# Hybrid diffusion step on one core: where the attention probabilities are normalised

## The reference, cut to what matters

```python
def attend(q, k, v, mask, sink):
    s = jnp.einsum('bqkgd,bskd->bkgqs', q.astype(F32), k.astype(F32)) * (HEAD_DIM ** -0.5)
    if mask is not None:
        s = jnp.where(mask, s, -jnp.inf)
    sk = sink.astype(F32)[None, :, :, None, None]
    m = jnp.maximum(jnp.max(s, axis=-1, keepdims=True), sk)
    e = jnp.exp(s - m)
    prob = e / (jnp.sum(e, axis=-1, keepdims=True) + jnp.exp(sk - m))
    o = jnp.einsum('bkgqs,bskd->bqkgd', prob, v.astype(F32))
    return o.astype(q.dtype)
```

## Time and profile before

| | |
|---|---|
| median of 3 runs | 2896.82 us (2895.7 to 2900.62) |
| the profiled execution | 2894.71 us, its span 2892.9 us |
| TensorE busy | 92% of the span |
| VectorE busy | 43% |
| ScalarE busy | 28% |
| GpSimd busy | 9% |
| DMA, mean | 74 GB/s |

### The profile page before, as it was taken

The page is one execution under the profiler, slowest core; times in us unless marked ns, Lnnn a source line. Parts: engine busy times, 40 slices in busy tenths (PEclk is TensorE's granted clock), DMA queues, the critical chain, the costliest instruction groups (busy, mean ns, idle before and its releaser), DMA issues.

```text
span 2892.9 us, 38685 instructions
## 1 busy us (share of the span) xinstructions
PE 2675.1 (92%) x16849; PEld 2314.2 (80%) x16849; DVE 1252.3 (43%) x1978; ACT 801.5 (28%) x1234; POOL 264.3 (9%) x174
## 2 busy tenths in 40 slices
PE   6989897889999899999988998788999998999998
PEld 4946445679999799999977564385899988999997
DVE  3495646452233422223356756636422343223224
ACT  5222122352224522112252211224321244221212
POOL 0020412000111000000001204210001110000000
PEclk8989998899999999999999999988999999999999
DMA  6021003223323032323302010122232221222221
GB/s 241 19 78 44 29 15 90 73 75 117 96 81 102 17 104 88 103 93 98 91 30 78 4 59 15 44 75 75 80 124 89 83 78 41 77 66 81 69 88 41
DMA packets 214622, 213.42 MB, mean 74 GB/s; under 512 B 29480, under 2 KB 205040, under 8 KB 214070
## 3 DMA queue, kind: packets, MB, share of 16 engines
q1 hardware_dynamic: 214454, 210.95, 23.2%
HBM read 207.52 MB, written 3.41 MB: 73 GB/s over the span
## 4 chain that ended last, share of the span: by engine, by line
PE 81%; DVE 12%; ACT 4%; issue 2%; POOL 1%; DMA 1%; SPq 0%; DVEq 0%; ACTq 0%
PE ps L622 54%; PE ps L581 6%; DVE arena L1614 4%; PE ps L605 3%; PE ps L1100 3%; PE ps L593 3%; PE ps L672 1%; PE ps L882 1%; DVE arena L1715 1%; PE ps L1010 1%; ACT normed L723 1%; DVE normed L748 1%; PE ps L1165 1%; PE ps L1260 1%; ACT arena L2081 1%
## 5 line engine op out<-in xcount | busy, mean ns | idle before, releaser
L622 PE MATMUL ps<-arena_parts,weights_parts 128*128 128x320 f32 x8416 | 1428.9, 309 | 3.6 <-DVE normed_parts L1689 3.6
L622 PEld LDWEIGHTS ps<-arena_parts,weights_parts 128*128 128x128 f32 x8416 | 1275.8, 187 | 19.2 <-DVE normed_parts L1689 4.4
L539 DVE TENSOR_TENSOR weights_parts<-weights,weights_parts 128x2048 fp32r<-128x2048 f32 (+2 forms) x140 | 285.5, 2039 | 772.5 <-ACT weights_parts L531 772.5
L622 PE MATMUL ps<-normed_parts,weights_parts 128*128 128x320 f32 x2240 | 510.0, 309 | 0.0
L622 PEld LDWEIGHTS ps<-normed_parts,weights_parts 128*128 128x128 f32 x2240 | 376.1, 188 | 0.0
L531 ACT CAST weights_parts<-weights 128x2048 fp32r<-128x2048 f32 (+2 forms) x140 | 232.5, 1660 | 267.8 <-PE ps L622 171.5
L581 PE MATMUL ps<-normed,weights 128*128 128x320 f32 x768 | 214.9, 439 | 6.2 <-DVE arena L1597 5.5
L581 PEld LDWEIGHTS ps<-normed,weights 128*128 128x128 f32 x768 | 146.2, 192 | 77.2 <-issue 20.5
L605 PE MATMUL ps<-arena_parts 128*128 128x320 f32 x448 | 104.8, 340 | 51.8 <-DVE arena_parts L755 19.8
L605 PEld LDWEIGHTS ps<-arena_parts 128*128 128x128 f32 x448 | 81.1, 209 | 60.4 <-DVE arena_parts L755 27.4
L2280 POOL TENSOR_TENSOR arena<-arena 128x640 f32<-128x640 f32 x32 | 54.4, 1699 | 787.6 <-DVE arena L1789 783.2
(11 more groups left out here) (261 smaller groups left out, 2586.3 us busy)
## 6 DMA issues: line engine op xcount, KB each, us to landing
weights<-in_w_in_dram SPq DMA_DIRECT2D x48, 1024.0 KB, 5.3
weights<-in_ada_w_dram SPq DMA_DIRECT2D x40, 1024.0 KB, 5.4
weights<-in_ffn_w_gate_dram SPq DMA_DIRECT2D x22, 1024.0 KB, 5.3
weights<-in_ffn_w_up_dram SPq DMA_DIRECT2D x22, 1024.0 KB, 5.3
weights<-in_ffn_w_down_dram SPq DMA_DIRECT2D x24, 768.0 KB, 4.4
weights<-in_w_out_dram SPq DMA_DIRECT2D x8, 1024.0 KB, 5.1
weights<-in_w_in_dram SPq DMA_DIRECT2D x66, 64.0 KB, 2.1
arena<-in_ada_w_dram SPq DMA_DIRECT2D x2, 2048.0 KB, 15.5
```

Of the source, the lines that this page charges most:

```text
L539: Vc(dve.tensor_tensor(part_view(m, 1), raw_view(n), part_view(m, 0).bitcast(F32), ALU.subtract) .then_inc(vector_done, 1), "part", m)
L622: m = pe.matmul(tokens(s)[0:cols, lo:hi], a[:, k, oc], x[k][:, lo:hi], start=k == 0 and i == 0, stop=k == n - 1 and i == 2)
```

## The change

The two multiplications by the reciprocal leave VectorE's `softmax_scale`, which now ends with the reciprocal (named "sums"). ScalarE gets a step `probs`, called here P(n): two `sc.mul` with the reciprocal as a per-partition operand, in place in `S_sb`. Its order in step n is now E(n), P(n-1), C(n-2). T(n) waits for P(n) on ScalarE's semaphore. The wait of `branch_high(0)` for the last probabilities is dropped.

```diff
                 def turn_probs(n):
                     b, t = UNITS[n]
-                    pe.wait_ge(vector_done, Vc["probs", n])
+                    pe.wait_ge(scalar_done, Sc["probs", n])
                     s = take(pe, "S", "PT", n)
...
                 def softmax_scale(n):
-                    b, _ = UNITS[n]
-                    w = n_keys(b) * P
                     dve.wait_ge(scalar_done, Sc["exp", n])
                     Vc(dve.tensor_tensor(stat[:, n, 6:8], stat[:, n, 6:8], stat[:, n, 4:6], ALU.add).then_inc(vector_done, 1))
                     dve.wait_ge(vector_done, Vc.count)
-                    Vc(dve.reciprocal(stat[:, n, 8:10], stat[:, n, 6:8]).then_inc(vector_done, 1))
-                    dve.wait_ge(vector_done, Vc.count)
-                    for g in range(2):
-                        Vc(dve.tensor_scalar(S_sb[n % 3][:, g, 0:w], S_sb[n % 3][:, g, 0:w], stat[:, n, 8 + g:9 + g], None, ALU.mult)
-                           .then_inc(vector_done, 1), "probs", n)
+                    Vc(dve.reciprocal(stat[:, n, 8:10], stat[:, n, 6:8]).then_inc(vector_done, 1), "sums", n)
...
+                def probs(n):
+                    b, _ = UNITS[n]
+                    w = n_keys(b) * P
+                    sc.wait_ge(vector_done, Vc["sums", n])
+                    for g in range(2):
+                        Sc(sc.mul(S_sb[n % 3][:, g, 0:w], S_sb[n % 3][:, g, 0:w], stat[:, n, 8 + g:9 + g])
+                           .then_inc(scalar_done, 1), "probs", n)
...
                 for n in range(len(UNITS) + 2):
                     if n < len(UNITS):
                         exps(n)
+                    if 1 <= n <= len(UNITS):
+                        probs(n - 1)
                     if n >= 2:
                         probs_turned(n - 2)
...
                 def branch_high(b):
                     if b == 0:
-                        sc.wait_ge(vector_done, Vc["probs", len(UNITS) - 1])
                         sc.wait_ge(tensor_done, Tn["att", len(UNITS) - 1])
```

## The result

The changed kernel takes 2929.5 us (median of 4 runs, 2926.8 to 2931.9) against 2896.3 for the kernel before (2895.6 to 2900.6): ratio 1.0111, 95% interval 1.0094 to 1.0129. It is 33 us slower; forecast were 24. A second set of runs gives 2928.9 and 1.0117 (1.0102 to 1.0132).

What follows compares the result with a forecast made beforehand. A loop of waits through all three engines, not any engine's share, was taken to bound attention. Stretch-by-stretch delays summed to 12.2 us per layer, +24.4 for two, giving 2920 us; range 2910 to 2930, widened to 2904 to 2936.

Steps and rivals of the forecast that it cites:

- What bounds the stage: Attention stage, 80.4 us per layer: a loop of waits through TensorE, VectorE and ScalarE, 6.75 us for two four-tile units.
- The price of the pair: Two ScalarE multiplications at 512 columns, priced from the exponentials: 1.24 us, bounds 0.98 to 1.44.
- The new loop: Four-tile units: TensorE's transposes wait for ScalarE's multiplications, delaying the next scores; 8.16 us for two units against 6.75.
- The sum up to unit 19: Added time per layer, stretch by stretch from unit 0 to 19, ahead of the tail's +1.3 in a 12.2 us total.
- 4 to 7: Stretch between the exponentials of units 4 and 7: 8.29 us against 7.91, +0.38 per layer.
- The tail: From unit 19's exponentials to the stage's end: 6.85 us against 5.58, +1.3 per layer.
- rival 3: TensorE's granted clock stays at 0.5 through the attention stage: 16 us a layer, 2951 us; chance 0.10.
- the prediction's own sign: Forecast wrong if four-tile exponentials still start every 3.1 to 3.6 us, or the clock shows 0.5 there.
- 81% busy in the loop: Argument against a falling clock: the new loop keeps TensorE busy 3.29 of 4.08 us.
- Rival 1: The multiplications hide in ScalarE's idle time and VectorE's chain share goes, 2.5 us a layer: 2890 us; chance 0.05.
- Rival 2: Loss is the difference of the two engines' pair times over all units, 12 us: 2907 us; chance 0.08.
- Rival 4: Each multiplication step needs ScalarE table loads, 102 us over 40 units: 3021 us; chance 0.02.

Runs made afterwards that it cites:

- x_again: The changed kernel run once more without any alteration, for the spread of its profile: 2928.9 us.
- b_early: Kernel before with TensorE's order alone altered, the scores issued one step early: 2904.0 us, ratio 1.0040.
- x_none: Changed kernel with the multiplications left out altogether, transposes waiting for the exponentials (results not those of the reference): 2891.7 us, ratio 0.9986.
- b_aside: Kernel before, VectorE still scaling, with the same two multiplications added on ScalarE, their products read by nobody: 2918.1 us, ratio 1.0073.
- x_warm2: Changed kernel with extra transposes of a constant on TensorE from unit 4 on, more of them at T(16) and S(18): 2921.9 us, ratio 1.0091.

## Why the prediction came out as it did

The mechanism was right; its size was short by 9 of 33 us, and 2929.5 lies at the very edge of the range 2910 to 2930. Up to unit 19 of an undisturbed stage the sum holds; what it lacks is TensorE's clock, in the tail and in mid-stage, and a cost outside the stages.

- What bounds the stage, the loop and not any engine's share: right. The price of the pair was 1.24 us, measured 1.23, and P at 512 columns takes 709 ns against E's 714.
- The new loop: 8.16 us forecast, 8.02 measured. Its terms are off both ways: the hand-over from P to TensorE is 0.04 for 0.21 and V 1.02 for 1.09, but P starts 1.62 behind E for 1.52, as it stands behind the sink's exponential.
- The sum up to unit 19, in excess over before, forecast then measured: 0 to 4 0.70, 0.52; 4 to 7 0.38, 0.85 (its clock was 0.98); 7 to 8 1.03, 1.02; 8 to 11 1.68, 1.56; 11 to 12 1.24, 1.22; 12 to 15 1.95, 1.79; 15 to 16 1.24, 1.23; 16 to 17 1.24, 1.22; 17 to 19 1.46, 1.41. Together 10.9 forecast and 10.8 measured; that it is this close is partly luck, as 0.47 too little between 4 and 7 makes up for the other eight, each 0.01 to 0.18 too long.
- The tail is the mis-sized term: +1.3 forecast, +2.7 measured in three of four stages (8.3 us; the clock is 0.79 over 8.21 us). TensorE waits 1.9 us for P(18) there. The order of work was right: in the fourth stage, the second of x_again, the clock is 1.00 and the tail 6.80 us, where the sum has 6.85. The error is that the sum took the clock at 1.00 there.
- Missing from the sum: the slow clock in mid-stage, which was rival 3 with 0.10 and the wrong form. It is not half clock throughout (2951 us) but a stretch of slow clock between units 8 and 12 that costs 3.6 us and comes in some stages: 2 of 4 here, none of 4 with fillers. Per execution that is some 4 us. By the prediction's own sign (wrong "if the clock shows 0.5 there") this part failed in one layer: clock 0.62 from unit 11 to 12. The argument against it, 81% busy in the loop, did not settle it, since the same program with the same work had the slow stretch in one layer and not in the other. What sets it off is not shown.
- Missing too: 4 us behind and between the stages, at unchanged code, in part at a slower clock (0.90 for 0.95 in the stretch shown above). They came in both executions of the changed kernel. The profiles of this study have between 1346.8 and 1350.7 us between the stages (before 1347.0), and they fall in two groups: all nine with multiplications on ScalarE have 1349.0 or more, all five without have 1348.5 or less, b_early with its longer stages among them at 1346.8. So this cost goes with P; by what way is open.
- 13.5 + 13.5 + 4 for one slow stretch + 4 outside is 35; the median difference is 33. So of the 9 us that the forecast lacks, the outside cost and the mid-stage stretch are some 4 each and the tails 3, which is 2 too many: the parts are known no better than that.

Rival 1, P hidden, fell with x_none and b_aside: the work wasn't hidden, and there was only 4 us to gain. Rival 2, plain exchange, names 12 us and fails by 21. Rival 4, a table load for P, did not come: the trace has the same 14 ACT_TABLE_LOADs before and after, none of them in the attention stages. The Trainium skill's rule ("ScalarE: Activation LUTs", "Rules for kernel authors": `mul` on VectorE) gives the right sign; the difference of 0.88 to 1.23 us in a pair, summed over the units as rival 2 does, is under half of the loss, the rest is the place in the loop and the clock.

## What to carry to other kernels

Idle time of an engine is room only behind the last instruction that somebody waits for: work put ahead of it delays that one, however idle the engine is afterwards. Whether that delay costs anything depends on which loop is the bound: with S one step early the same 20 us of work a layer cost 0.1 and 3.0 us in the stages. Before moving work off an engine, ask what its removal alone is worth (here 4 us of 2896), which one kernel without it measures. And when an order is changed, write out every loop it closes: the order that made one kernel 8 us faster made the other 10 us slower.

## What the runs showed of the hardware

- Extra transposes on TensorE made the changed kernel faster by 4 and 7 us. Behind TensorE's waits of 6.0 us for P(16) and 1.9 us for P(18) the granted clock was 0.53 (units 17 to 19) and 0.79 (tail); with fillers in these waits (x_warm2) it was 1.00 in both stretches, and they took 7.06 and 7.15 us for 9.16 and 8.28.
- Two executions of one program had the same slow stretch (12.5 and 9.0 us at clock 0.86 and 0.62), equal to 0.02 us, in different layers.
